# First mixer: early modulation tiles in places of their own, another order of parts and turnings, later tiles loaded sooner and summed one tile later

## The chip, the core and the metric

The kernel runs on one core of a Trainium2 chip. The metric is the device time of one execution in microseconds (us). TensorE is called PE here (its weight loads PEld), VectorE DVE, ScalarE ACT, GpSimd POOL, and SyncE SP; SP issues nearly all transfers from HBM. A "line" such as L1755 is a line of the kernel before, if nothing else is said.

## What is computed

Two transformer-like blocks on 256 tokens of width 1024 in float32. The change touches only the first thing that the kernel does: the modulation vectors and the first mixer up to its gates. Cut to that part:

```python
mod = jax.nn.silu(c) @ w_mod[i] + b_mod[i]            # 1024 -> 6144
sh1, sc1, g1, sh2, sc2, g2 = jnp.split(mod[:, None, :], N_MOD, axis=-1)
mod_c = jax.nn.silu(c_ctx) @ w_mod[i] + b_mod[i]      # the same for the context
h_lat = rms_norm(x_lat, norm1_g[i]) * (1.0 + sc1) + sh1
h_ctx = rms_norm(x_ctx, norm1_g[i]) * (1.0 + csc1) + csh1
...
q, v, zf, zb, g = jnp.split(h @ w_in, N_HG_PROJ, axis=-1)   # h: both, 512 rows
x_lat = x_lat + g1 * y_lat                                  # y_lat: the mixer's output
h2_lat = rms_norm(x_lat, norm2_g[i]) * (1.0 + sc2) + sh2    # then experts, then block two
```

## The kernel before

There is no scheduler: each engine's program is written out by hand, in order, and semaphores join them. An engine that waits holds everything behind it in its own program, and this is also true of SP, whose program is the list of transfers.

**Weight tiles.** All weights of the projections come as tiles of 1 MB (128 x 2048 float32) through three places, `raw0` to `raw2`. For each, ACT makes a rounded copy `whi` (L1244), DVE the rest `wlo` (L1755), and PE multiplies with both (three matmuls for each product). `whi` and `wlo` have four places each, and the split of a tile is written three tiles ahead of its use (`take`). A tile's load waits until the tile before it in the same place has been split. Counted from the first projection, weight tiles 0 to 3 are q (48 matmuls of 256 columns each), 4 to 7 are v (48 matmuls of 512 columns each), 8 and 9 are the first gates z0 and z1, and so on.

**Early modulation.** Columns 0 to 2047 of `w_mod` (sh1 and sc1) are eight 1 MB tiles. They are items of the same list, go through the same three places ahead of weight tile 0, and are used whole: PE multiplies the four rows of `CS` with them (`mod_rows`, L655, part c = 0 to 3 with two tiles each), ACT copies the 4 x 512 result out (L1338), PE turns it (`mod_cols`, L664) and DVE sums and adds the bias. PE turns the latent rows (`X`) and the context rows (`XC`) with `norm` (L642), ACT squares them (L1255), DVE scales (L1953), modulates (L1960) and, with ACT (L1270) and POOL (L2544), splits them into `HH` and `HL`. Then q0 may start.

**Later modulation.** Columns 2048 to 5119 are twelve 1 MB tiles, here called modulation tiles 0 to 11, in four places of their own in `ARENA` (`MRAW`, `load_mod`, L501). ACT multiplies a tile in place by the vector c (`products`, four instructions at L1318). When two neighbouring tiles (2s, 2s+1) are done, POOL adds them in three instructions (`row_sums`, L2557, L2559, L2562). This document calls the six results S4 to S9, by their column block: S4 comes from tiles 0 and 1, S5 from 2 and 3, S6 from 4 and 5, up to S9 from 10 and 11. PE folds each over the partitions (`mod_sums`, L676 for S4 and S5, L674 for the others) and DVE takes it over (`mod_cols`, L1867 or L1862). Modulation tiles 4 and 5 go to the places of 0 and 1, and their load therefore waits for S4; 6 and 7 wait for S5, 8 and 9 for S6, 10 and 11 for S7.

**The end of v.** The v projection fills banks 0 to 3 in weight tiles 4 and 5. Before tile 6 may start, DVE must have copied banks 0 and 2 (L2015), and ACT 1 and 3 (L1365). In DVE's program the copies stand behind the split of weight tile 8 and the take-over of S5.

**The gates.** ACT's first gate `unit_gate(0)` (L1288) waits for S9 and z0; z1 needs banks that it frees.

The two lines that tie the streams are, in SP's and POOL's programs:

```python
elif n >= 4:
    sp.wait_ge(*pmod.at("tile", n - 4))      # load_mod: n-4 is freed by its sum
...
if i == 14 or 16 <= i < 20:                  # i counts the 8 early tiles too:
    n = 2 if i == 14 else 2 * i - 28         # weight tile 6 behind modulation tiles 2, 3;
    load_mod(n)                              # 8 behind 4, 5; 9 behind 6, 7; ...
    load_mod(n + 1)
```

Of the kernel before, what the change touches and what calls it, by code (L numbers as in the profile page):

```python
# [114 lines left out]
MOD_SUMS = ((4,), (5,), (6,), (7,), (8, 9))  # L115
# [3 lines left out]
def weights(I):  # L119
# [14 lines left out]
    wm, wi = I["w_mod"][0], I["hg_w_in"][0]  # L134
    whole = set()

    def mod(c):
        whole.update((len(items), len(items) + 1))
        plan(wm, 0, 4, 512 * c, 512)
        plan(wm, 4, 4, 512 * c, 512)  # L140
# [7 lines left out]
    for c in range(4):  # L148
        mod(c)
# [68 lines left out]
    return items, base, whole  # L218


def build(nc, I, out, table):

    with ExitStack() as ctx:
# [19 lines left out]
        s_ld = [sem(f"raw{i}_landed") for i in range(NR + 2)]  # L243
        first, rows, xin, consts = (Landed(sem(n)) for n in ("first_landed", "rows_landed", "x_landed", "consts_landed"))
        gateb, router, fgl = (Landed(sem(n)) for n in ("gate_landed", "router_landed", "final_g_landed"))
# [28 lines left out]

        items, base, whole = weights(I)
        split_items = [i for i in range(len(items)) if i not in whole]
        turn_of = {i: n for n, i in enumerate(split_items)}


# [14 lines left out]
        due, n = [], NS - 1  # L294
        for i in range(len(items)):
            before = sum(1 for j in split_items[:n] if j < i)
            due.append([])
            while (n < len(split_items) and n < before + NS
                   and all(w < i for w in whole if w <= split_items[n] - NR)):
                due[i].append(n)  # L300
                n += 1
# [4 lines left out]
        for k, group in enumerate(PARAMS):  # L306
            r = 0
            for what, n in group:
                col.setdefault(what, at + r)
                r += n  # L310
            pt.append((ar(5000 if k == 0 else 7000 + 128 * k, 128), r, at))
            at += r
# [11 lines left out]
        FT, FTC = eight(ar(2048, 2048)), eight(ar(8192, 2048))  # L324
# [6 lines left out]
        MRS = [MR[:, :], ar(5400, 512)[0:4, :]]  # L331
# [19 lines left out]
        MRAW = [ar(o, 2048) for o in (10240, 6144, 8192, 12288)]  # L351
        MACC = [ar(14336, 512), G2B[:, 0:512]]
# [113 lines left out]
        def sync_program(sp):  # L466
            state, moe = {}, base["moe"]

            def load(i):
# [8 lines left out]
                if held[i] is not None:  # L478
                    sp.wait_ge(*(prj.at("item", held[i]) if held[i] in whole else wlow(held[i])))
                elif place[i] >= NR:  # L480
                    sp.wait_ge(*mm.at("mod_late", 11, 1))
                sp.dma_start(raw[place[i]][:, :].rearrange("p (k n) -> p k n", k=nk), src).then_inc(s_ld[place[i]], 16)

            def load_mod(n):
# [6 lines left out]
                elif n == 1:  # L491
                    sp.wait_ge(*vps.at("columns", 4))
                elif n == 2:
                    sp.wait_ge(*vlo.at("n", "hg_c", 2))
                    sp.wait_ge(*plo.at("n", "hg_c", 3))
                elif n == 3:
# [9 lines left out]

            sp.dma_start(CST[:, C_ID:C_ID + 128], I["consts"][:, C_ID:C_ID + 128]).then_inc(*first())
# [54 lines left out]
        def tensor_program(pe):  # L562
            state = {"next": 0, "late": 0}

            def take():
# [3 lines left out]
                if i in whole:  # L569
                    pe.wait_ge(s_ld[place[i]], 16 * had[i])  # L570
                    return i, [raw[place[i]][:, :].rearrange("p (k n) -> p k n", k=nk)]
                pe.wait_ge(*wlow(i))
                return i, [w[turn_of[i] % NS][:, :].rearrange("p (k n) -> p k n", k=nk) for w in (whi, wlo)]
# [59 lines left out]
            def norm(stage, xs, before=None, late=False):  # L633
                for q in range(4):
# [3 lines left out]
                    b = banks.next(pe, RING, "norm", stage, q)  # L638
# [9 lines left out]
            def mod_rows(c):  # L648
                b = banks.next(pe, SIDE, "mod_rows", c)
                if c == 0:  # L650
                    pe.wait_ge(*vec.at("cs"))
                for half in range(2):
                    i, (w,) = take()
                    for k in range(4):
                        x = pe.matmul(bank[b][0:4, :], f32(CSv[:, 4 * half + k, :]), w[:, k, :], start=half == 0 and k == 0,  # L655
                                      stop=half == 1 and k == 3)
                    x.then_inc(*prj("item", i))
                prj.also("mod_rows", c)

            def mod_cols(c):  # L660
                b = banks.next(pe, SIDE, "mod_cols", c)
                pe.wait_ge(*act.at("mod_rows", c))
                for k in range(4):
                    x = pe.transpose(bank[b][:, 4 * k:4 * k + 4], MRS[c % 2][:, 128 * k:128 * k + 128], ident[0:4, 0:4])  # L664
# [97 lines left out]
            def hgrn():  # L762
# [3 lines left out]
                pe.wait_ge(*xin.all(4))  # L766
                norm("hg_x", X, late=True)
# [1877 lines left out]
```

## Time and profile before

| | |
|---|---|
| three runs, median (lowest to highest) | 2089.04 us (2087.76 to 2092.61) |
| the profiled execution | 2090.62 us |
| its span in the trace | 2089.0 us |
| first matmul of the projections (q0) | 59.93 us after the span's start |
| first matmul of weight tile 6 | 121.29 us |
| first matmul of z1 | 159.88 us |

Between the profiled execution's time and its span lie 1.6 us. All times of the trace are counted from the span's start. In rows of a timeline the columns are start, duration, engine, line, operation, out<-in, shape and count, and in square brackets how long the engine sat idle and what ended it. "Chain" rows are the work that ended last, followed back: start, duration, what.

### The profile page before, as it was taken

To read this page: it belongs to the slowest core of one execution; us is meant where nothing else is said; L and a number is where in the kernel's file an instruction comes from. 1 tells how busy PE (TensorE), PEld (TensorE's weight loads), DVE (VectorE), ACT (ScalarE), POOL (GpSimd) and SP (SyncE) were. 2 spreads that over 40 slices of the span, in tenths; PEclk is the share of its full clock that TensorE was granted. 3 is DMA by queue.
4 is the path that set the end of the run, shared out by engine and by line. 5 is a ranking of instruction groups with operands and counts; after the bars stand their busy time and mean duration, and the time that the engine had idled before them with its cause. 6 is when DMAs were issued, how large, how long until landed. Compare 5 with 4: busy or idle time off the path is not lost.

```text
span 2089.0 us, 29140 instructions
## 1 busy us (share of the span) xinstructions
PE 1972.5 (94%) x12305; PEld 1737.2 (83%) x12305; DVE 1313.9 (63%) x1599; ACT 1036.7 (50%) x1211; POOL 89.7 (4%) x42
## 2 busy tenths in 40 slices
PE   7799989999989999999988999999999999999998
PEld 2678888698979888999877899897799988888997
DVE  1637765578876466665697655646655575567554
ACT  2656764377764455433535433445433344555332
POOL 0390000000000000000000000000000000000000
PEclk9899999899999999999999999999999999999999
DMA  6681125398964544565430456551365555345562
GB/s 233 245 300 42 60 80 195 102 343 301 308 214 162 181 142 161 165 199 182 151 121 22 160 182 194 173 182 61 104 197 183 194 170 181 122 161 180 183 191 82
DMA packets 230060, 355.55 MB, mean 170 GB/s; under 512 B 7058, under 2 KB 179883, under 8 KB 229675
## 3 DMA queue, kind: packets, MB, share of 16 engines
q1 hardware_dynamic: 229378, 353.47, 51.3%
q8 instruction: 98, 1.61, 0.3%
q10 hardware_dynamic: 552, 0.22, 0.0%
q14 instruction: 32, 0.25, 0.0%
HBM read 352.62 MB, written 1.05 MB: 169 GB/s over the span
## 4 chain that ended last, share of the span: by engine, by line
PE 83%; DVE 8%; ACT 4%; DMA 2%; issue 1%; POOL 0%; SPq 0%; ACTq 0%; DVEq 0%; POOLq 0%
PE bank L576 12%; PE bank L577 12%; PE bank L578 12%; PE bank L593 11%; PE bank L594 11%; PE bank L595 11%; DVE wlo L1755 2%; PE bank L1101 2%; ACT whi L1244 1%; DVE ARENA L2367 1%; DMA raw<-in_hg_w_in 1%; PE bank L655 1%; ACT ARENA L1255 1%; PE bank L858 1%; PE bank L837 1%
## 5 line engine op out<-in xcount | busy, mean ns | idle before, releaser
L1755 DVE TENSOR_TENSOR wlo<-raw,whi 128x2048 fp32r<-128x2048 f32 x282 | 653.2, 2320 | 348.2 <-ACT whi L1244 347.8
L1244 ACT CAST whi<-raw 128x2048 fp32r<-128x2048 f32 x282 | 535.4, 1903 | 224.8 <-PE bank L578 205.6
L593 PE MATMUL bank<-HH,whi 128*128 128x256 f32 (+1 forms) x2048 | 605.6, 296 | 15.3 <-DVE HL L1802 9.4
L594 PE MATMUL bank<-HL,whi 128*128 128x256 f32 (+1 forms) x2048 | 597.5, 292 | 0.0
L595 PE MATMUL bank<-HH,wlo 128*128 128x256 f32 (+1 forms) x2048 | 597.3, 292 | 0.0
L593 PEld LDWEIGHTS bank<-HH,whi 128*128 128x128 f32 x2048 | 397.1, 194 | 27.8 <-issue 14.0
L594 PEld LDWEIGHTS bank<-HL,whi 128*128 128x128 f32 x2048 | 397.3, 194 | 8.9 <-issue 1.9
L595 PEld LDWEIGHTS bank<-HH,wlo 128*128 128x128 f32 x2048 | 396.7, 194 | 5.1
L576 PE MATMUL bank<-whi,YH 128*128 128x512 f32 x816 | 320.8, 393 | 7.0 <-DVE YL L2411 5.6
L577 PE MATMUL bank<-wlo,YH 128*128 128x512 f32 x816 | 319.2, 391 | 0.0
L578 PE MATMUL bank<-whi,YL 128*128 128x512 f32 x816 | 318.1, 390 | 0.0
L576 PE MATMUL bank<-whi,HH 128*128 128x256 f32 (+1 forms) x544 | 183.4, 337 | 6.3 <-DVE ARENA L2015 3.1
L576 PEld LDWEIGHTS bank<-whi,YH 128*128 128x128 f32 x816 | 153.9, 189 | 37.5 <-DVE YL L2411 6.0
L578 PEld LDWEIGHTS bank<-whi,YL 128*128 128x128 f32 x816 | 153.7, 188 | 32.7
L578 PE MATMUL bank<-whi,HL 128*128 128x256 f32 (+1 forms) x544 | 179.0, 329 | 0.0
L577 PE MATMUL bank<-wlo,HH 128*128 128x256 f32 (+1 forms) x544 | 179.0, 329 | 0.0
L1531 ACT ACTIVATE YH<-ARENA 128x512 fp32r<-128x512 f32 x64 | 40.6, 634 | 278.6 <-DVE ARENA L2253 278.6
L577 PEld LDWEIGHTS bank<-wlo,YH 128*128 128x128 f32 x816 | 154.0, 189 | 28.4
L576 PEld LDWEIGHTS bank<-whi,HH 128*128 128x128 f32 x544 | 104.1, 191 | 21.8 <-issue 10.1
L577 PEld LDWEIGHTS bank<-wlo,HH 128*128 128x128 f32 x544 | 104.2, 192 | 9.6 <-issue 0.5
L578 PEld LDWEIGHTS bank<-whi,HL 128*128 128x128 f32 x544 | 104.1, 191 | 9.3
L2544 POOL TENSOR_TENSOR HL<-ARENA,HH 128x512 fp32r<-128x512 f32 x20 | 28.1, 1409 | 1799.4 <-ACT HH L1270 1799.4
(361 smaller groups left out, 1921.5 us busy)
## 6 DMA issues: line engine op xcount, KB each, us to landing
raw<-in_ffn_w SPq DMA_DIRECT2D x128, 1024.0 KB, 5.5
raw<-in_ret_w_in SPq DMA_DIRECT2D x48, 1024.0 KB, 5.2
raw<-in_hg_w_in SPq DMA_DIRECT2D x20, 1024.0 KB, 5.3
ARENA<-in_w_mod SPq DMA_DIRECT2D x16, 1024.0 KB, 7.5
raw<-in_ret_w_out SPq DMA_DIRECT2D x16, 1024.0 KB, 5.0
raw<-in_moe_w_gate SPq DMA_DIRECT2D x13, 1024.0 KB, 7.2
raw<-in_moe_w_up SPq DMA_DIRECT2D x13, 1024.0 KB, 7.4
raw<-in_moe_w_down SPq DMA_DIRECT2D x12, 1024.0 KB, 7.4
```

The lines of the kernel that those rows point to most:

```text
L576: pe.matmul(ps, lh, rh, start=start, stop=False)
L577: pe.matmul(ps, lh, rl, start=False, stop=False)
L578: return pe.matmul(ps, ll, rh, start=False, stop=stop)
L593: pe.matmul(ps, w[0][:, k, c], ah, start=begin, stop=False, skip_group_check=True)
L594: pe.matmul(ps, w[0][:, k, c], al, start=False, stop=False, skip_group_check=True)
L595: x = pe.matmul(ps, w[1][:, k, c], ah, start=False, stop=k == 7, skip_group_check=True)
L655: x = pe.matmul(bank[b][0:4, :], f32(CSv[:, 4 * half + k, :]), w[:, k, :], start=half == 0 and k == 0, stop=half == 1 and k == 3)
L1101: x = pe.matmul(bank[bf][:, c:c + 256], DG[:, n % NDG, :], HP[:, f, w:w + 256], start=w == (9 if f == 5 else 0), stop=w == 30)
L1244: ac.copy(whi[n % NS][:, :], raw[place[i]][:, :]).then_inc(*whi_("w", i))
L1531: ac.activation(yslot(j)[0], TG[j % 2], ACT.Square).then_inc(*ahi(st, "y", j))
L1755: ve.tensor_tensor(wlo[n % NS][:, :], raw[place[i]][:, :], f32(whi[n % NS][:, :]), SUB).then_inc(*wlv("w", i))
L2544: po.tensor_tensor(dst[1][:, kk, :], ft[:, kk, :], f32(dst[0][:, kk, :]), SUB).then_inc(*plo("n", stage, q))
```

## The change

What it does, part by part:

1. The eight early tiles of `w_mod` are no longer items of the weight list. They get eight places (`MFIRST`: the three `raw` places and five stretches of `ARENA`) and are all issued at the start, without waits. `raw` is first given to weight tiles once `mod_rows` has read it.
2. The order of the four parts is 0, 2, 1, 3 (`MOD_FIRST`): the first halves of shift and scale come first, and DVE normalizes and modulates the first half of the columns ahead of the second. The latent rows (`X`) wait for themselves alone. The context rows are loaded behind weight tile 0, turned on PE behind q0, and scaled and modulated on DVE behind the split of weight tile 3; all four of their low parts are on DVE, none on POOL.
3. The constants row groups 1 to 4 (`columns`) are turned ahead of the second part.
4. Modulation tiles 0 to 3 are loaded ahead of weight tile 4, and tiles 4 and 5, 6 and 7, 8 and 9, 10 and 11 each ahead of weight tiles 6, 7, 8 and 9.
5. ACT's `products`: tiles 0, 1 behind q0 (before: behind q2), 2, 3 behind q1 (q3), 4, 5 behind q3, where the split of weight tile 6 stands right ahead (before: behind the split of tile 7), then 6, 7 behind the split of tile 7, 8, 9 behind tile 8's and 10, 11 behind tile 9's.
6. PE folds S4 ahead of weight tile 4 (before: behind it), S5 behind tile 4, S6 behind 5, S7 behind 6, S8 behind 7, S9 behind z0.

The core of the diff:

```diff
-MOD_SUMS = ((4,), (5,), (6,), (7,), (8, 9))
+MOD_FIRST = (0, 2, 1, 3)
+MOD_SUMS = ((4,), (5,), (6,), (7,), (8,), (9,))
...
+        MFIRST = [r[:, :] for r in raw[0:3]] + [ar(o, 2048) for o in (0, 10240, 6144, 8192, 4096)]
...
             load_rows(sp, 0, first)
-            for i in range(NR):
-                load(i)
+            load_first(0)
+            load_first(1)
             for i in range(2):
                 sp.dma_start(X[i], I["x"][0, 128 * i:128 * i + 128, :]).then_inc(*xin())
+            load_first(2)
+            load_first(3)
+            load(0)
             for i in range(2):
-                sp.dma_start(XC[i], I["ctx"][0, 128 * i:128 * i + 128, :]).then_inc(*xin())
-            for i in range(NR, 13):
-                load(i)
+                sp.dma_start(XC[i], I["ctx"][0, 128 * i:128 * i + 128, :]).then_inc(*cin())
+            load(1)
             load_mod(0)
             load_mod(1)
+            load(2)
+            load_mod(2)
+            load(3)
             sp.dma_start(CST[:, 128:], I["consts"][:, 128:C_END]).then_inc(*consts())
+            load_mod(3)
+            for i in range(4, 6):
+                load(i)
...
-            for i in range(13, len(items)):
-                if i == 14 or 16 <= i < 20:
-                    n = 2 if i == 14 else 2 * i - 28
+            for i in range(6, len(items)):
+                if 6 <= i < 10:
+                    n = 2 * i - 8
                     load_mod(n)
                     load_mod(n + 1)
...
                 for j in range(4):
                     proj_b(("q", j), H16, 256, "hg_x" if j == 0 else None)
-                pe.wait_ge(*vlo.at("n", "hg_c", 2))
-                pe.wait_ge(*plo.at("n", "hg_c", 3))
+                    if j == 0:
+                        pe.wait_ge(*cin.all(2))
+                        norm("hg_c", XC, late=True, apart=SIDE)
+                        rms_rows("hg_c")
+                pe.wait_ge(*consts.all(1))
+                for n in MOD_SUMS[0]:
+                    mod_sums(n)
+                pe.wait_ge(*vlo.at("n", "hg_c", 3))
...
-                        for n in MOD_SUMS[2 * c + half]:
+                        for n in MOD_SUMS[2 * c + half + 1]:
                             mod_sums(n)
...
-                    if j == 0:
+                    if j == 2:
                         norm("hg_c", HC, shifted=True, late=True, ft=FTC)
-                    if j >= 2:
-                        products(2 * j - 4)
-                        products(2 * j - 3)
+                    if j != 2:
+                        n = (0, 1, 1, 2)[j]
+                        products(2 * n)
+                        products(2 * n + 1)
                 for c in range(2):
                     for half in range(2):
                         take()
-                        products(4 + 4 * c + 2 * half)
-                        products(5 + 4 * c + 2 * half)
+                        if 2 * c + half < 3:
+                            products(6 + 4 * c + 2 * half)
+                            products(7 + 4 * c + 2 * half)
```

The front of ACT's program, behind the first part's copy:

```diff
+                mod_out(0)
+                ac.wait_ge(*xin.all(2))
                 sum_squares(X, "hg_x")
                 rstd("hg_x")
+                mod_out(1)
+                mod_out(2)
+                normed(0)
+                normed(1)
+                split(0)
+                ac.wait_ge(*cin.all(2))
                 sum_squares(XC, "hg_c", 4)
...
+                mod_out(3)
+                normed(2)
+                normed(3)
                 split(1)
                 split(2)
+                rstd("hg_c")
```

**Where instructions stand, before and now.** SP's program from weight tile 5 on, before (a load with 4x512 into `raw` is a v tile, one with 8x256 a gate tile, one into `ARENA` a modulation tile; `pool_modulation` is POOL's sum):

```order
L482 DMA raw1<-in_hg_w_in 128x4x512 [waits dve_weight_lo]
L501 DMA ARENA<-in_w_mod 128x4x512 [waits pool_lo,dve_lo]
L501 DMA ARENA<-in_w_mod 128x4x512 [waits act_other,pe_transpose]
L482 DMA raw2<-in_hg_w_in 128x4x512 [waits dve_weight_lo]
L482 DMA raw0<-in_hg_w_in 128x4x512 [waits dve_weight_lo]
```

SP's program now, behind the load for `SM`:

```order
L485 DMA ARENA<-in_w_mod 128x4x512 [waits pool_modulation] x2
L469 DMA raw0<-in_hg_w_in 128x4x512 [waits dve_weight_lo]
L485 DMA ARENA<-in_w_mod 128x4x512 [waits pool_modulation] x2
L469 DMA raw1<-in_hg_w_in 128x4x512 [waits dve_weight_lo]
L485 DMA ARENA<-in_w_mod 128x4x512 [waits pool_modulation] x2
L469 DMA raw2<-in_hg_w_in 128x8x256 [waits dve_weight_lo]
```

Weight tiles 6 and 7 (the two last rows before, raw0 and raw1 now) stood ahead of the first wait for POOL; now tile 6 stands behind one pair that waits for POOL, tile 7 behind two, and tile 8 (raw2, 8x256) behind three. Before, tile 8 stood behind one.

ACT's program from the products of modulation tiles 2 and 3 on, before (`mod0` to `mod3` are the four places of modulation tiles; `whi` and `raw` numbers are places):

```order
L1318 ACTIVATE ARENA<-ARENA,SM 128x512 [waits mod3_landed]
L1318 ACTIVATE ARENA<-ARENA,SM 128x512 x3
L1244 CAST whi3<-raw0 128x2048 [waits pe_project,raw0_landed]
L1318 ACTIVATE ARENA<-ARENA,SM 128x512 [waits mod0_landed]
L1318 ACTIVATE ARENA<-ARENA,SM 128x512 x3
L1318 ACTIVATE ARENA<-ARENA,SM 128x512 [waits mod1_landed]
```

ACT's program now, from behind q2's silu on:

```order
L1270 CAST HH<-ARENA 128x2x256 [waits dve_other] x4
L1245 CAST whi2<-raw0 128x2048 [waits pe_project,raw0_landed]
L1364 ACTIVATE ARENA<-bank5 128x512 [waits pe_project]
L1318 ACTIVATE ARENA<-ARENA,SM 128x512 [waits mod0_landed]
L1318 ACTIVATE ARENA<-ARENA,SM 128x512 x3
L1318 ACTIVATE ARENA<-ARENA,SM 128x512 [waits mod1_landed]
```

The products of tiles 4 and 5 stood behind the split of weight tile 7 (whi3 from raw0); now they stand behind the split of weight tile 6 (whi2 from raw0) and q3's silu.

DVE's program around the copies out of banks 0 and 2, before:

```order
L1755 TENSOR_TENSOR wlo3<-raw0,whi3 128x2048 [waits act_weight_hi]
L1867 TENSOR_TENSOR G1B<-G1B,bank5 128x512 [waits gate_landed,pe_transpose]
L1755 TENSOR_TENSOR wlo0<-raw1,whi0 128x2048 [waits act_weight_hi]
L1867 TENSOR_TENSOR G1B<-G1B,bank6 128x512 [waits gate_landed,pe_transpose]
L2015 COPY ARENA<-bank0 128x512 [waits pe_project]
```

and now:

```order
L1769 TENSOR_TENSOR wlo3<-raw1,whi3 128x2048 [waits act_weight_hi]
L1879 TENSOR_TENSOR G1B<-G1B,bank7 128x512 [waits gate_landed,pe_transpose]
L1769 TENSOR_TENSOR wlo0<-raw2,whi0 128x2048 [waits act_weight_hi]
L1874 TENSOR_TENSOR SM<-bank4,PRM 128x4 [waits pe_transpose]
L2046 COPY ARENA<-bank0 128x512 [waits pe_project]
```

In both the copy stands behind the split of weight tile 8 (into wlo0); the sum that is taken over between them is now S6 (L1874) and was S5 (L1867).

## Rows read from the trace of the kernel before

**Rows 1.** The page: its span and busy time.
```profile
span 2089.0 us, 29140 instructions
PE 1972.5 (94%) x12305; PEld 1737.2 (83%) x12305; DVE 1313.9 (63%) x1599; ACT 1036.7 (50%) x1211; POOL 89.7 (4%) x42
```

**Rows 2.** Waits of PE from 60 to 260 us: total, times, longest.
```profile
PE bank L676 <- POOL ARENA L2562: 6.8, 1, 6.8
...
PE bank L576 <- DVE ARENA L2015: 3.1, 1, 3.1
```

**Rows 3.** Timeline of PE: early parts, a turning, q0, z1.
```profile
9.65 8.53 PE L655 MATMUL bank<-raw,CS 128*4 128x512 f32 x16 [3.82 <-DMA raw<-in_w_mod]
...
36.16 1.97 PE L642 MATMUL bank<-CST,ARENA 128*128 128x128 f32 x16
...
46.32 7.03 PE L655 MATMUL bank<-raw,CS 128*4 128x512 f32 x16
...
59.93 0.55 PE L593 MATMUL bank<-HH,whi 128*128 128x256 f32 x1 [5.45 <-DVE HL L1967]
...
159.88 0.47 PE L593 MATMUL bank<-HH,whi 128*128 128x512 f32 x1 [0.52 <-ACT ARENA L1289]
```

**Rows 4.** Busy time in a stretch of 5 us: five engines, clock, DMA share, GB/s.
```profile
15.00:20.00 5.00, 3.18 (x8) 0.52 (x6) 0.00 (x0) 0.00 (x0) 0.00 (x0) 1.00 1.03 379
```

**Rows 5.** Timeline of ACT: silu of q0, products of modulation tiles 0, 1 and 4.
```profile
76.89 0.60 ACT L1351 ACTIVATE ARENA<-bank 128x512 f32<-128x512 f32 x1
...
87.08 5.00 ACT L1318 ACTIVATE ARENA<-ARENA,SM 128x512 f32<-128x512 f32 x8
...
107.76 2.57 ACT L1318 ACTIVATE ARENA<-ARENA,SM 128x512 f32<-128x512 f32 x4 [5.30 <-DMA ARENA<-in_w_mod]
```

**Rows 6.** The chain that ended last, from 0 to 260 us: start, duration, what.
```profile
22.75 0.73 ACT ARENA L1255 x2
...
134.05 0.79 PE bank L674 x8
...
145.89 0.79 PE bank L674 x8
```

**Rows 7.** The same chain, from 92 to 122 us.
```profile
92.16 4.61 POOL ARENA L2557
...
96.84 4.28 POOL ARENA L2559
...
101.20 1.28 POOL ARENA L2562
...
103.46 9.91 DMA raw<-in_hg_w_in
...
113.39 1.93 ACT whi L1244
...
115.38 4.49 issue
...
120.54 0.61 DVE ARENA L2015
...
121.29 0.47 PE bank L576
```

**Rows 8.** Timeline of DVE: splits, the context's modulation.
```profile
56.90 2.28 DVE L1755 TENSOR_TENSOR wlo<-raw,whi 128x2048 fp32r<-128x2048 f32 x1
...
66.73 2.67 DVE L1960 TENSOR_SCALAR ARENA<-ARENA,SM 128x256 f32<-128x256 f32 x8
...
115.34 4.61 DVE L1755 TENSOR_TENSOR wlo<-raw,whi 128x2048 fp32r<-128x2048 f32 x1 [9.96 <-ACT whi L1244]
```

**Rows 9.** Timeline of POOL: its additions of S5 and S6.
```profile
109.31 2.40 POOL L2559 TENSOR_TENSOR ARENA<-ARENA 128x1024 f32<-128x1024 f32 x1
...
113.19 4.60 POOL L2557 TENSOR_TENSOR ARENA<-ARENA 128x2048 f32<-128x2048 f32 x1
117.87 4.30 POOL L2559 TENSOR_TENSOR ARENA<-ARENA 128x1024 f32<-128x1024 f32 x1
```

More of the change, by code:

```diff
@@ L273, in build @@
         twice = lambda ap: ap.rearrange("p (m n) -> p m n", m=1).to_broadcast([128, 2, 256])
-        items, base, whole = weights(I)
-        split_items = [i for i in range(len(items)) if i not in whole]
-        turn_of = {i: n for n, i in enumerate(split_items)}
+        items, base = weights(I)
         place, held, had, turns, newest = [], [], [], list(range(NR)), {}
@@ L293, in build @@
             had.append(place.count(turns[-1]))
[L294 to L301, printed above, removed]
         wlow = lambda i: wlv.at("w", i)
@@ L568, in take @@
                 nk = items[i][1]
-                if i in whole:
-                    pe.wait_ge(s_ld[place[i]], 16 * had[i])
-                    return i, [raw[place[i]][:, :].rearrange("p (k n) -> p k n", k=nk)]
                 pe.wait_ge(*wlow(i))
-                return i, [w[turn_of[i] % NS][:, :].rearrange("p (k n) -> p k n", k=nk) for w in (whi, wlo)]
+                return i, [w[i % NS][:, :].rearrange("p (k n) -> p k n", k=nk) for w in (whi, wlo)]
             def mm3(ps, lh, ll, rh, rl, start, stop):
@@ L631, in rms_rows, with norm @@
                 x.then_inc(*mm("rms", stage))
-            def norm(stage, xs, before=None, late=False):
+            def norm(stage, xs, before=None, late=False, apart=()):
                 for q in range(4):
@@ L646, in norm, with mod_rows, mod_cols @@
                     rms_rows(stage)
-            def mod_rows(c):
+            def mod_rows(j):
+                c = MOD_FIRST[j]
                 b = banks.next(pe, SIDE, "mod_rows", c)
-                if c == 0:
+                if j == 0:
                     pe.wait_ge(*vec.at("cs"))
[L652 to L660, printed above, removed]
+                pe.wait_ge(s_modf[j], 32)
+                for k in range(8):
+                    w = MFIRST[2 * j + k // 4][:, 512 * (k % 4):512 * (k % 4) + 512]
+                    x = pe.matmul(bank[b][0:4, :], f32(CSv[:, k, :]), w, start=k == 0, stop=k == 7)
+                x.then_inc(*prj("mod_rows", c))
+            def mod_cols(j):
+                c = MOD_FIRST[j]
                 b = banks.next(pe, SIDE, "mod_cols", c)
@@ L777, in hgrn @@
                     columns(k)
+                mod_rows(1)
+                pe.wait_ge(*xin.all(2))
+                norm("hg_x", X, late=True)
+                mod_cols(0)
+                mod_cols(1)
+                mod_rows(2)
+                rms_rows("hg_x")
                 mod_rows(3)
@@ L1759, in take @@
                 for _ in range(count):
-                    i = state["next"]
                     state["next"] += 1
-                    for n in due[i]:
-                        split(n)
+                    split(state["next"] + NS - 2)
             def own(ins):
@@ L1968, in low_part, with scales_of @@
                         *vlo("n", stage, q))
-                take(8)
-                normalized(0)
-                normalized(1)
-                mod_cols(0)
-                mod_cols(1)
+                def scales_of(half):
+                    for v in range(2):
+                        o = 8 * v + 4 * half
+                        sc = MODT[:, 1, :].rearrange("p (t v) -> p v t", v=2)[:, v, 4 * half:4 * half + 4]
+                        own(ve.scalar_tensor_tensor(MS[:, o:o + 4], sc, 1.0, prm("norm1_g", 4 * half, 4), ADD, MUL))
                 for k in range(1, 5):
                     columns(k)
+                rstd("hg_x", "hg_x")
+                mod_cols(0)
                 mod_cols(2)
-                mod_cols(3)
-                for v in range(2):
-                    sc = MODT[:, 1, :].rearrange("p (t v) -> p v t", v=2)[:, v, :]
-                    own(ve.scalar_tensor_tensor(MS[:, 8 * v:8 * v + 8], sc, 1.0, prm("norm1_g", 0, 8), ADD, MUL))
+                scales_of(0)
+                ve.wait_ge(*mm.at("rms", "hg_x"))
+                ve.tensor_copy(RBC[:, :], bank[0][:, 0:256]).then_inc(*vps("rms", "hg_x"))
+                banks.free(("rms", "hg_x"), vps)
+                ve.wait_ge(*vps.last())
+                normalized(0)
                 modulated(0, 0)
@@ L1989, in hgrn @@
                 split(1)
-                for q in range(4):
-                    modulated(1, q)
                 split(2)
@@ L2004, in hgrn @@
                 take()
-                low_part(1, 0)
-                low_part(1, 2)
-                take(3)
+                ve.wait_ge(*mm.at("rms", "hg_c"))
+                ve.tensor_copy(RBC[:, :], bank[0][:, 0:256]).then_inc(*vps("rms", "hg_c"))
+                banks.free(("rms", "hg_c"), vps)
+                ve.wait_ge(*vps.last())
+                normalized(1)
+                for q in range(4):
+                    modulated(1, q)
+                take(2)
+                for q in range(4):
+                    low_part(1, q)
+                take()
+                for n in MOD_SUMS[0]:
+                    mod_cols(n)
                 for c in range(2):
@@ L2010, in hgrn @@
                         take()
-                        for n in MOD_SUMS[2 * c + half]:
+                        for n in MOD_SUMS[2 * c + half + 1]:
                             mod_cols(n)
```

116 lines of the change are left out of this document (55 added, 61 removed).

## The prediction

> **What bounds the kernel now.** I read the page first: PE is busy 94% of 2089.0 us [rows 1], so a change to the start can give or take only idle time of PE, and the rest of the program follows as a block. I place the end of what the change touches at the first matmul of z1, 159.88 us [rows 3]. Behind it no instruction changes its place, and both kernels need S9 and z0 there. So the sum is: by how much does that matmul move?
>
> Next the waits of PE and its timeline. Ahead of q0 PE is tied to the early modulation and the scaled rows: q0 starts at 59.93 after 5.45 us of waiting for DVE [rows 3]. Behind it there are two waits worth counting: 6.8 us for POOL's S4, and 3.1 us for DVE's copy out of bank 0 [rows 2]. The second looks small, but the chain that ended last runs through it [rows 7]: POOL's three instructions of S4 (92.16 to 102.48), then the transfer of weight tile 8, then its rounding on ACT, its rest on DVE, the copy, and weight tile 6 on PE at 121.29. A DVE copy that needs nothing but v0 and v1 stands behind a weight tile that had to queue behind two modulation tiles, and those had waited for POOL. From the end of S4 to PE's start it is 121.29 - 102.48 = 18.8 us: 10.9 to the landing (113.39 is where ACT starts on the tile), 1.9 on ACT, 4.6 on DVE, and 1.3 for S5's take-over and the copy.
>
> **Part 1, the start: a gain.** PE takes the first early tile at 9.65 [rows 3]; the rest follow at 379 GB/s [rows 4], 2.8 us for each 1.05 MB. The first part now waits for both tiles, 12.4 us, and takes 8.5 us as in the row with the cold start, the three others 7.0 each [rows 3]. Their tiles are there in time (the eighth at about 32 us, the fourth part begins about 39). With some 4 us of turnings among them (2.0 for X [rows 3], the others smaller) the last part ends at 12.4 + 8.5 + 21.1 + 4 = 46 us, before at 53.35. ACT, however, now has the split of weight tile 0 and the four squares of the context (4 x 0.73 [rows 6]) ahead of the last part's copy; I put q0 at 50.5 us, 9.4 earlier.
>
> **Part 2, POOL's start: a larger gain.** Products of modulation tiles 0 and 1 ended at 92.08, POOL began at 92.16 [rows 5, 7]. Silu of q0 was at 76.89 [rows 5], 23.5 us behind the last part's end. In that stretch the change adds the squares (+2.9) and a second root (+0.8), takes the context's modulation out (-2.7 [rows 8]), and moves the first half's scaling, modulation and split under the last part (-2.3 for the split [rows 8], about -2 for the rest). That leaves 20.3, so silu of q0 is at about 66.5, and with 0.6 and 5.0 us behind it [rows 5] the products end near 72 to 73.4. POOL's S4 costs 4.6 + 2.4 + 1.3 = 8.3 us undisturbed. It was 10.3, because DVE's split and POOL's addition do not overlap: POOL's 2.40 becomes 4.30, and DVE's 2.28 becomes 4.61 while POOL is in its 4.60 [rows 8, 9]. Now two splits (weight tiles 4 and 5) and the context's four low parts fall into S4. Undisturbed S4 would end at 81.7, with every DVE instruction ahead of POOL at 88. The rows show both sides waiting, so I take two splits: 86.0. That is 16.5 us sooner than 102.48.
>
> **Part 3, the order of loads: the loss.** The copy out of bank 0 still stands behind the split of weight tile 8. But tile 8 now stands in SP's program behind modulation tiles 8 and 9, which wait for S6; before it stood behind 4 and 5, which wait for S4. And S6 has moved away from S4. Its products (tiles 4 and 5) stand on ACT behind the rounding of weight tile 6, whose load in turn stands behind modulation tiles 4 and 5 on SP. Step by step from the end of S4, with the durations of before:
>
> - three tiles issued and landed, the weight tile last: 10.9 us [rows 7]
> - ACT rounds weight tile 6: 1.9 [rows 7]; silu of q3: 0.6; products of 4 and 5: 5.1 [rows 5]. Before, they ran at 107.76, as soon as the modulation tile had landed [rows 5]
> - POOL's S6: 8.3, and 2.2 more for one split (tile 7) in it; hand-overs 0.1
>
> So S6 = S4 + 29.2 (27.0 with no split in it) = 115.2. Then the same trip a second time: 10.9 to the landing of weight tile 8, 1.9 on ACT, 2.3 on DVE (POOL waits for products then, so I take the undisturbed price; with it in the way 4.6), 1.0 for S6's take-over and the copy: 16.1 us. Weight tile 6 starts on PE at 131.3, 10.0 us **later** than 121.29. PE needs v0 and v1 ahead of it: S4's fold at 87, the context's low parts about 89, then twice 11.05 us (145.89 - 134.05 - 0.79 [rows 6]) and the folds. That is about 115: PE would stand some 16 us, and what PE gained at the start is idle time here.
>
> From weight tile 6 to z1 the work is the same: tiles 6, 7 and z0, two folds between them (0.79 each [rows 6]), the slow first matmuls after a wait in both. S9 was no limit before; now it ends near 153, ahead of z0's end, near 168. So z1 moves by +10.0.
>
> The trip is also where the Trainium skill has a price of its own. "DMA: Bandwidth & Descriptors", section on the anatomy of one DMA, puts a transfer at about 2.0 us plus its bytes over 436 GB/s. An estimate from it for three tiles in a row is 9.2 us instead of the measured 10.9; over two trips the change would cost 3.4 us less, 2095.6. The page's fit is for transfers that GpSimd issues, and the row is this queue's own, so the measured one is in the sum.
>
> **The sum.** Only PE's last link counts: -16.5 (S4) + 29.2 (S6 behind S4) + 16.1 (second trip) - 18.8 (the one trip of before) = +10.0 us. Against the profiled execution, 2090.62 (1.6 more than its span), that is 2100.6; against the median of the runs, 2089.04, it is **2099.0 us**.
>
> The parts with one answer: the turning of the constants is the same four instructions earlier; all eight places for early tiles cost no instruction; four low parts on DVE instead of two are 1.4 us on an engine that then waits for weight tile 6 anyway; the new wait for the root of the context ahead of q1 holds PE for 1 to 2 us, hidden by the stand further on.
>
> **Rivals.**
>
> *Faster.* The long chain does not hold PE, because POOL or the queue is much quicker than I put it, and PE is bound by its own work. Then tile 6 starts near 113 to 115, and z1 moves by -6 to -8: 2082. For it: everything ahead of S4 is earlier. Against it: tile 6 starts ahead of 121.29 only if S6 is done by 105.2, thus S4 by 78.2 even with no split inside S6. The products alone end at 72, and 8.3 must follow. The Trainium skill's rule of thumb (the same page, rules for kernel authors) is to issue a DMA early, so that its cost overlaps; by it the earlier modulation tiles would be this gain. Here a tile issued early is a tile that others queue behind. I give this 7%.
>
> *About the same, or slightly slower.* The chain holds as I say, but DVE and POOL hardly meet: S4 ends at 81.7, S6 27.0 later, tile 6 at 124.8. With the start 1 us quicker too, z1 moves by +2.5: 2091.5. I give results within 4.2 us of the median 11% in all. For it: POOL's six sums were never all disturbed (one 2.40 among them). Against it: two splits must fall in S4, because S4 starts just as weight tile 4 has been rounded.
>
> *Still slower.* DVE keeps ahead of POOL through its low parts (S4 at 88), and the split of tile 8 meets POOL (4.6): +14.3, 2103. I give it 20%, inside "slower".
>
> *The change does not do what it says.* If q0 did not start earlier, because ACT or the row constants are late, all of it would slide by up to 9 more. I see no wait in the listing for that: 3%.
>
> **Numbers.** Chances: my forecast (2095 to 2102) 59%, still slower 20%, the last rival 3%, about the same 11%, faster 7%. A measurement of this kernel can tell about 0.2%, 4.2 us, from no change. Faster by more than that: 0.07; within it: 0.11; slower: 0.82. The range of 80% reaches from 2091 (no meeting of POOL and DVE) to 2104.
>
> **What the profile would show.** Right: q0 at 49 to 52 us; S4's last POOL instruction ending at 83 to 88; ACT idle for some 15 us ahead of rounding weight tile 6 and again ahead of tile 8; weight tile 6 of PE waiting over 10 us for the DVE copy, at 129 to 133; z1 at 167 to 172. Wrong: if that copy is not the last thing that tile 6 waits for, if modulation tiles do not delay the weight tile behind them by about 5 us, or if POOL is idle for less than 5 us ahead of S6. And if tile 6 starts late as I say but the time is not longer, then PE caught up further on, which I have excluded.

## The result, and the profile after

| | before | after |
|---|---|---|
| median (lowest to highest), 7 runs each | 2089.05 us (2087.72 to 2092.61) | 2095.12 us (2092.75 to 2097.82) |
| after / before | | 1.0028, 95% interval 1.0017 to 1.0040 |
| the profiled execution, and its span | 2090.62, 2089.0 us | 2095.05, 2093.7 us |
| first matmul of q0 | 59.93 us | 49.43 us |
| last instruction of S4 on POOL ends | 102.48 us | 82.26 us |
| first matmul of weight tile 6 | 121.29 us | 126.57 us |
| first matmul of z1 | 159.88 us | 165.17 us |

The change makes the kernel 6.1 us slower. The forecast was 10.0 us slower, 2099.0, with a range that holds 2095.1. The table already tells the story: 10.5 us won at q0, 20.2 us won at S4, and 5.3 us lost at weight tile 6.

The first matmuls of q0 and of z1 in PE's timeline after (compare [rows 3]):

```profile
49.43 0.39 PE L589 MATMUL bank<-HH,whi 128*128 128x256 f32 x1
...
165.17 0.47 PE L589 MATMUL bank<-HH,whi 128*128 128x512 f32 x1 [0.43 <-DVE SM L1874]
```

The page after (compare [rows 1]): PE does the same matmuls, and the span is longer.

```profile
span 2093.7 us, 29142 instructions
PE 1968.0 (94%) x12305; PEld 1733.5 (83%) x12305; DVE 1323.3 (63%) x1603; ACT 1035.9 (49%) x1211; POOL 83.6 (4%) x40
```

The waits of PE after, from 50 to 260 us (total, times, longest; compare [rows 2]):

```profile
PE bank L572 <- DVE HL L1979: 9.9, 1, 9.9
PE bank L572 <- DVE ARENA L2046: 6.7, 1, 6.7
...
PE bank L675 <- POOL ARENA L2593: 4.4, 1, 4.4
```

Three waits take the place of two (6.8 and 3.1 before). L572 is the v projection: PE waits 9.9 us for the context's low parts ahead of v0, and 6.7 us for the copy out of bank 0 ahead of weight tile 6; 4.4 us are for S4, ahead of its fold. The chain that ended last, after, shows where the wait of 6.7 us comes from (start, duration, what; compare [rows 7]):

```profile
71.52 4.80 POOL ARENA L2588
76.39 2.40 POOL ARENA L2590
78.86 3.40 POOL ARENA L2593
...
83.26 9.56 DMA raw<-in_hg_w_in
...
95.23 4.91 ACT ARENA L1318 x8
100.28 4.59 POOL ARENA L2588
104.95 2.41 POOL ARENA L2590
107.43 3.23 POOL ARENA L2593
...
111.64 9.87 DMA raw<-in_hg_w_in
121.53 1.91 ACT whi L1245
123.46 2.29 DVE wlo L1769
125.83 0.61 DVE ARENA L2046
126.57 0.76 PE bank L572
```

Read it from the top. POOL makes S4; its end lets SP issue modulation tiles 4 and 5, and behind them weight tile 6 (the DMA at 83.26). ACT must round that tile before its products of 4 and 5 (95.23). Then POOL makes S6, SP issues 8 and 9 and behind them weight tile 8 (111.64), ACT and DVE split it, and only then comes the copy that PE waits for. The round trip "sum, transfer, ACT" stands in the chain twice. Before it stood there once.

### The profile page after: what moved, and what is told of

Same layout as the page of the kernel before. It is cut to its first block, busy times and chain, and to the rows that moved or that the text cites. A ratio compares the mean times of both kernels' runs of the same rounds, so it can differ in the third digit from the quotient of the medians.

```text
span 2093.7 us, 29142 instructions
## 1 busy us (share of the span) xinstructions
PE 1968.0 (94%) x12305; PEld 1733.5 (83%) x12305; DVE 1323.3 (63%) x1603; ACT 1035.9 (49%) x1211; POOL 83.6 (4%) x40
## 4 chain that ended last, share of the span: by engine, by line
PE 81%; DVE 9%; ACT 5%; DMA 2%; issue 2%; POOL 1%; SPq 0%; ACTq 0%; DVEq 0%; POOLq 0%
PE bank L572 12%; PE bank L573 12%; PE bank L574 12%; PE bank L589 11%; PE bank L590 11%; PE bank L591 11%; DVE wlo L1769 3%; PE bank L1103 2%; ACT whi L1245 2%; DVE ARENA L2398 1%; PE bank L655 1%; ACT ARENA L1255 1%; DMA raw<-in_hg_w_in 1%; PE bank L860 1%; PE bank L839 1%
## 5 line engine op out<-in xcount | busy, mean ns | idle before, releaser
L572 PE MATMUL bank<-whi,YH 128*128 128x512 f32 x816 | 320.8, 393 | 7.0 <-DVE YL L2442 5.6
L572 PE MATMUL bank<-whi,HH 128*128 128x256 f32 (+1 forms) x544 | 183.6, 337 | 20.1 <-DVE HL L1979 9.9
L572 PEld LDWEIGHTS bank<-whi,YH 128*128 128x128 f32 x816 | 153.9, 189 | 37.5 <-DVE YL L2442 6.0
L572 PEld LDWEIGHTS bank<-whi,HH 128*128 128x128 f32 x544 | 104.3, 192 | 36.3 <-DVE HL L1979 11.5
L2284 DVE SCALAR_TENSOR_TENSOR ARENA<-bank,RBC 128x512 f32<-128x512 f32 x64 | 44.2, 691 | 86.6 <-PE bank L591 86.4
```

Of the source, the lines that this page charges most:

```text
L572: pe.matmul(ps, lh, rh, start=start, stop=False)
L2284: ve.scalar_tensor_tensor(tr, two(bank[b][:, :]), 0.0, rbc2, ALU.max, MUL).then_inc(*vps(st, j))
```

## The experiments

Six of the eight kernels start from one of the two kernels and change one or two things. e5 changes several at once, and e8 adds one thing to e5. z1 is the first matmul of z1 in the profiled execution; its shift is against 159.88. Each ratio is against runs of the kernel before on the same chip; e8 ran on another chip than e1 to e7.

| | z1 starts | shift of z1 | median | ratio to before (95%) |
|---|---|---|---|---|
| after | 165.17 | +5.3 | 2095.12 | 1.0028 (1.0017 to 1.0040) |
| e1, load order of before | 156.84 | -3.0 | 2086.41 | 0.9991 (0.9982 to 1.0000) |
| e2, copies ahead | 157.05 | -2.8 | 2088.76 | 1.0000 (0.9991 to 1.0009) |
| e7, both | 156.48 | -3.4 | 2087.98 | 0.9994 (0.9985 to 1.0004) |
| e3, products ahead | 161.80 | +1.9 | 2092.70 | 1.0018 (1.0009 to 1.0027) |
| e4, before with the new load order | | | 2160.21 | 1.0341 (1.0322 to 1.0360) |
| e6, e1 with one low part | 153.50 | -6.4 | 2083.15 | 0.9969 (0.9957 to 0.9982) |
| e5, context first | 150.30 | -9.6 | 2079.52 | 0.9954 (0.9941 to 0.9968) |
| e8, e5 with S9 on DVE | 145.05 | -14.8 | 2075.04 | 0.9929 (0.9916 to 0.9943) |

The times follow z1, but only to within 3 us. In the profiled executions the span moves by up to 2.1 us more or less than z1 does, and each median, against the runs of before beside it, comes out 0.5 to 2.8 us later than the shift of z1 says.

**e1: the load order alone.** The changed kernel, with the pairs of modulation tiles where they stood before, two weight tiles later:

```diff
-                if 6 <= i < 10:
-                    n = 2 * i - 8
+                if 8 <= i < 12:
+                    n = 2 * i - 12
```

> The changed kernel with one part undone: modulation tiles 4 to 11 are loaded ahead of weight tiles 8 to 11 again, so weight tiles 6 and 7 wait for no sum. Theory (the chain S4, loads, products 4 and 5, S6, loads, weight tile 8, DVE's copy holds weight tile 6 on PE): tile 6 starts on PE right behind v1, at about 118.9 us instead of 126.57, and the time falls by 7.7 us, to about 2087.4. Rival (the loss comes from DVE and POOL blocking each other, v0 starting late): v0 still starts at 94 and the time stays within 2 us of 2095.

Measured: 2086.41 us (2085.50 to 2090.68). In e1's waits of PE the copy is down to 0.9 us, and weight tile 6 starts at 120.85 (theory 118.9). The copy's wait, then the first matmul of v0 in its timeline:

```profile
PE bank L572 <- DVE ARENA L2046: 0.9, 1, 0.9
```
```profile
94.58 0.79 PE L572 MATMUL bank<-whi,HH 128*128 128x512 f32 x1 [9.96 <-DVE HL L1979]
```

So the wait for the copy is nearly gone, and the one ahead of v0 is there as in the changed kernel. The order of loads accounts for the whole loss: undoing it gives back 8.7 us. What is left of the change gains 2.5 us, which the interval (up to 1.0000) only just tells from nothing. It gains no more since v0 starts at 94.6, and PE then runs through v0 and v1 to the copies.

**e2 and e7: the copy alone, and both.** In e2 the load order stays, and DVE and ACT copy the banks of v ahead of the split of weight tile 8 instead of behind it (and ahead of that of tile 10):

```diff
                     for half in range(2):
+                        if half:
+                            ve.wait_ge(*prj.at("v", c))
+                            ... copies out of banks 0 and 2 (ACT: 1 and 3)
                         take()
```

> The changed kernel with its load order, but the copies out of banks 0 to 3 stand on DVE and ACT ahead of the split of weight tile 8 (and of tile 10) instead of behind it. Theory: the late landing of tile 8, near 121 us, no longer reaches PE; tile 6 starts near 119 and z0 (144) still comes after the split of tile 8 (126): about 2087.5. Rival (the loads themselves are late for PE, or POOL's S9 is the bound): 2093 to 2095.

Measured: 2088.76 us (2086.68 to 2090.41). In PE's waits the copy is missing altogether, and weight tile 8 still is issued late, in SP's timeline of e2 at 112.57 us:

```profile
111.61 0.92 SPq L485 DMA_DIRECT2D ARENA<-in_w_mod  x2
112.57 0.51 SPq L469 DMA_DIRECT2D raw<-in_hg_w_in  x1
```

So the late tile costs only through the copy that stands behind its split. e7 makes both edits:

> e1's load order and e2's earlier copies together in the changed kernel. Theory: they cut the same chain, so together they bring no more than one: tile 6 was already right behind v1 in both, only DVE's last 0.9 us goes: 2085.5 to 2088.5. Rival (two separate losses of some 6 to 8 us each): near 2080.

Measured: 2087.98 us (2087.03 to 2088.86). Each edit takes z1 from +5.3 to about -3, both together to -3.4. They cut the same chain at two links, and what bounds PE behind it is v0. z1 moved by -2.8 in e2, the median by -0.2 only; e1 kept 2.5 of its 3.0. The difference lies behind z1, and no run here explains it.

**e3: products ahead.** If the sum S6 is the trouble, ACT could make its products ahead of the split of weight tile 6:

```diff
                 for j in range(4):
+                    if j == 3:
+                        products(4)
+                        products(5)
                     take()
...
-                    if j != 2:
-                        n = (0, 1, 1, 2)[j]
+                    if j < 2:
+                        n = (0, 1)[j]
```

> The changed kernel with its load order, but ACT multiplies modulation tiles 4 and 5 ahead of rounding weight tile 6. Theory: the products run as soon as the tiles land (87.6 to 93), S6 ends at 103.5 instead of 110.7, weight tile 8 lands at 114.4 and the copy is done at 119.3; tile 6 starts near 119.6: about 2088. Rival (POOL's own time or the queue sets S6): S6 stays at 108 or later and the time above 2093.

Measured: 2092.70 us (2091.35 to 2094.40), a miss by 4.7 us. The chain did what was asked of it: S6 ended at 103.9 instead of 110.7. But now POOL has no pause between S5 and S6, and DVE loses by it. POOL and then DVE in e3:

```profile
82.05 6.43 POOL L2591 TENSOR_TENSOR ARENA<-ARENA 128x2048 f32<-128x2048 f32 x1
88.56 2.68 POOL L2593 TENSOR_TENSOR ARENA<-ARENA 128x1024 f32<-128x1024 f32 x1
91.32 1.59 POOL L2596 TENSOR_TENSOR G2B<-ARENA 128x512 f32<-128x512 f32 x1
93.00 4.83 POOL L2591 TENSOR_TENSOR ARENA<-ARENA 128x2048 f32<-128x2048 f32 x1
```
```profile
84.05 14.33 DVE L1982 TENSOR_TENSOR HL<-ARENA,HH 128x512 fp32r<-128x512 f32 x4
```

Four low parts, from 84.05 to 98.4, lie beside POOL's four additions of 82.05 to 97.8. PE waits for them 14.3 us instead of 9.9, and v0 starts at 98.43, 3.9 us later than in e1. Weight tile 6 starts at 125.80, 4.95 later than in e1; the last 1.1 us of that lie between v0 and tile 6 and were not traced.

**e4: the new load order in the kernel before.** The reverse of e1: pairs of modulation tiles ahead of weight tiles 5 to 9, and nothing else.

```diff
-                if i == 14 or 16 <= i < 20:
-                    n = 2 if i == 14 else 2 * i - 28
+                if 13 <= i < 18:
+                    n = 2 * i - 24
```

> The kernel before with one part done alone: the pairs of modulation tiles from 4 on stand two weight tiles earlier in SP's order (4, 5 ahead of weight tile 6, and so on; 2, 3 ahead of tile 5), nothing else. ACT's products of 2 and 3 stand behind the split of tile 6 here, so every sum waits for a weight tile that waits for the sum before. Theory: S4 at 102.5, tile 6 lands at 113.4, S5 near 131, S6 near 159, tile 8 lands near 170, weight tile 6 starts on PE near 176, and S9 near 227 holds the first gate: +55 to +70 us, 2145 to 2160. Rival (sooner loads are harmless or help): within 10 us of 2089.

Measured: 2160.21 us (2160.02 to 2160.40, two runs), 71 us slower, a little over the expected span. SP's timeline of e4:

```profile
82.20 0.93 SPq L501 DMA_DIRECT2D ARENA<-in_w_mod  x2
83.19 0.50 SPq L482 DMA_DIRECT2D raw<-in_hg_w_in  x1
109.61 0.92 SPq L501 DMA_DIRECT2D ARENA<-in_w_mod  x2
...
161.57 0.92 SPq L501 DMA_DIRECT2D ARENA<-in_w_mod  x2
```

and one turn of its chain:

```profile
83.19 10.75 DMA raw<-in_hg_w_in
...
96.37 4.89 ACT ARENA L1318 x8
101.33 4.50 POOL ARENA L2557
105.90 2.35 POOL ARENA L2559
108.32 1.27 POOL ARENA L2562
...
110.57 9.57 DMA raw<-in_hg_w_in
```

A pair is issued every 26.5 us (from 82.20 to 161.57 in three turns): transfer, split, products and sum in a ring. Weight tile 6 starts on PE at 177.96, after a wait of 39.9 us for the copy out of bank 0 (theory: near 176). In the kernel before, the products of tiles 4 and 5 stand behind the split of weight tile 7, those of 6 and 7 behind tile 8's; with the new load order that weight tile in turn stands behind a pair that waits for the sum just before. No two steps of the ring overlap. The changed kernel opens it by making each pair of products one split sooner, and is left with two turns ahead of the copy. The order of loads is worth as much as the order on ACT allows.

**e6: one instruction for the four low parts.** e1, and on DVE:

```diff
                 for q in range(4):
-                    low_part(1, q)
+                    ve.wait_ge(*ahi.at("n", "hg_c", q))
+                ve.tensor_tensor(HC[1], FTC, f32(HC[0]), SUB).then_inc(*vlo("n", "hg_c", 3))
```

> The kernel e1_loads_back (modulation pairs behind weight tiles 6 and 7) with one more edit: the context's four low parts on DVE, 128x512 each, are one instruction of 128x2048. With the loads back the next limit is the start of v0 at 94.6, held by the four low parts, which take 10.0 us for 2.7 us of work, since each of them waits for an addition of POOL. Theory (DVE pays per instruction, not per element, when POOL adds): one instruction waits once, is done near 91.3, v0 starts 3 us earlier and the time falls from 2086.4 to about 2083.5. Rival (the port is shared by the bytes moved): no change, 2086.

Measured: 2083.15 us (2079.97 to 2086.50). The rest of the context on DVE and v0 on PE, in e6:

```profile
84.50 6.58 DVE L2036 TENSOR_TENSOR HL<-ARENA,HH 128x2048 fp32r<-128x2048 f32 x1
```
```profile
91.14 0.80 PE L572 MATMUL bank<-whi,HH 128*128 128x512 f32 x1 [6.52 <-DVE HL L2036]
```

The same bytes take 6.58 us in one instruction and 10.02 in e1's four. v0 starts 3.4 us sooner, z1 3.3 us sooner, the median falls by 3.3 us. Here the price of meeting POOL was paid for each instruction, not for each byte.

**e5: the context ahead of POOL.** The load order of e1, the copies of e2, and: ACT's products of tile 1 wait until the context is rounded, so that DVE has modulated and split it before POOL begins; ACT's products of tiles 2 to 11 each stand one place later than in the changed kernel; PE folds S4 behind v1 instead of ahead of v0, and S5 to S8 one or two places later; the fourth early part's copy stands ahead of the context's squares on ACT. None of these was run alone.

```diff
-MOD_SUMS = ((4,), (5,), (6,), (7,), (8,), (9,))
+MOD_SUMS = ((), (4,), (5,), (6, 7), (8, 9))
...
-                    if j == 2:
+                    if j == 0:
+                        products(0)
                         norm("hg_c", HC, shifted=True, late=True, ft=FTC)
+                    if j == 1:
+                        products(1)
```

> A version built from what the runs showed: the changed kernel with the loads of e1, the copies out of banks 0 to 3 ahead of the splits of tiles 8 and 10, ACT's copy of the last early part ahead of the context's squares, the context's rounding and low parts done before POOL starts (ACT: products of tile 0, the context, split of tile 4, products of tile 1; DVE: low parts ahead of the splits of 4 and 5), and S4 folded behind v1 instead of ahead of v0. Theory: low parts end near 76, v0 starts right behind q3 at 78 to 80; POOL runs without a gap from about 78 to 142, S9 becomes the bound of the first gate, z1 starts near 144 instead of 159.9: about 2073. Rival (what was saved ahead is again lost behind, at another wait): above 2083.

Measured: 2079.52 us (2078.60 to 2080.63), faster than both kernels, but 6.5 us short of the time that was expected (about 2073). DVE's context work, in e5:

```profile
72.23 2.66 DVE L1972 TENSOR_SCALAR ARENA<-ARENA,SM 128x256 f32<-128x256 f32 x8
74.81 2.49 DVE L1979 TENSOR_TENSOR HL<-ARENA,HH 128x512 fp32r<-128x512 f32 x4
```

2.66 and 2.49 us, where the changed kernel has 9.14 and 9.99 (rows in the next section). v0 starts at 82.77 with no wait at all, 11.6 us sooner. Where did the rest go? The end of POOL's timeline and z1, in e5:

```profile
136.47 4.61 POOL L2590 TENSOR_TENSOR ARENA<-ARENA 128x2048 f32<-128x2048 f32 x1 [1.57 <-ACT ARENA L1316]
141.16 4.27 POOL L2592 TENSOR_TENSOR ARENA<-ARENA 128x1024 f32<-128x1024 f32 x1
145.50 1.26 POOL L2595 TENSOR_TENSOR G2B<-ARENA 128x512 f32<-128x512 f32 x1
```
```profile
150.30 0.77 PE L589 MATMUL bank<-HH,whi 128*128 128x512 f32 x1 [1.55 <-ACT ARENA L1287]
```

S9 was no limit before; here z0's products are done at 141.2 and the first gate stands until S9 ends at 146.76. POOL had begun at 80.38 and needs 66.4 us for the six sums, 12.4 for the first and 10.3 to 10.5 for each of the others, with hardly a pause.

**e8: S9 on DVE.** e5, with the three additions of the last sum on DVE, ahead of its last split there, and the gate's wait turned to them:

```diff
+                t0, t1, acc = MRAW[2], MRAW[3], MACC[1]
+                ve.wait_ge(*act.at("products", 11))
+                own(ve.tensor_tensor(t0, t0, t1, ADD))
+                own(ve.tensor_tensor(t0[:, 0:1024], t0[:, 0:1024], t0[:, 1024:2048], ADD))
+                own(ve.tensor_tensor(acc, t0[:, 0:512], t0[:, 512:1024], ADD))
+                vec.also("sums", 9)
                 take()
...
-            for c in range(4, 10):
+            for c in range(4, 9):
                 row_sums(c)
```

> The context-first version, with one thing changed: the last of the six sums (tiles 10 and 11) is made on VectorE instead of GpSimd, and the first gate unit waits for it there. In the context-first version's trace z0's products end at 141.6, but the sigmoids of z0 wait for GpSimd's last sum (136.47 to 146.76, three adds of 4.61, 4.27 and 1.26 us), so z1 starts at 150.30. Theory A (the 6 us that the context-first version fell short of its expectation, 2079.5 instead of 2073, are this wait, because GpSimd works back to back from 80.38 on and a sum takes 10.4 us there): on VectorE the three adds take an estimated 2.3 + 1.3 + 0.7 us (its rows of 128x2048 and 128x512) and end at 141, z1 starts at 143.5 to 145, and the time falls by 5 to 7 us, to 2072.5 to 2074.5. Theory B (the shortfall lies later in the program, in the places of the low granted clock, or the wait is only replaced, for instance by the split of z1's weight tile, which now stands behind the adds on VectorE): z1 starts later than 147 and the time stays within 2 us of 2079.5.

Measured: 2075.04 us (2070.07 to 2075.85). DVE and PE, in e8:

```profile
137.22 2.29 DVE L2053 TENSOR_TENSOR ARENA<-ARENA 128x2048 f32<-128x2048 f32 x1 [1.54 <-ACT ARENA L1317]
139.54 1.23 DVE L2054 TENSOR_TENSOR ARENA<-ARENA 128x1024 f32<-128x1024 f32 x1
140.80 0.69 DVE L2055 TENSOR_TENSOR G2B<-ARENA 128x512 f32<-128x512 f32 x1
```
```profile
145.05 0.77 PE L589 MATMUL bank<-HH,whi 128*128 128x512 f32 x1 [1.28 <-ACT ARENA L1288]
```

The sum takes 4.3 us instead of 10.3, z1 starts 5.25 us sooner, and the median falls by 4.5. Against the kernel before on its own chip, e5 is 9.1 us faster and e8 13.2, so the fall may be nearer 4.1. That is theory A in the main: z1 came at the late end of its range, and theory B had put it later than 147. But the fall is short of the 5 to 7 us that A gave; of the 6.5 us that e5 missed, some 2 stay unexplained. e8 is 13 us faster than the kernel before and 19 to 20 us faster than the changed one. It keeps the change's early tiles and early context; what it drops is the order of loads, and the order on ACT and DVE that let the sums meet the context.

## Why the prediction was right, and where it was off

The mechanism was right: the second trip through POOL, the queue and ACT is what makes weight tile 6 late. The size was too large, and the median came out only just inside the part of the range that I gave 59% (2095 to 2102). Of the profile's signs that I named, only the start of q0 came in its range. S4 ended at 82.26 (named: 83 to 88), weight tile 6 started at 126.57 (129 to 133) after a wait of 6.7 us (over 10), z1 at 165.17 (167 to 172), and ACT sat idle for 9.9 and 9.6 us ahead of weight tiles 6 and 8 (some 15). None of the signs of a wrong mechanism came: the copy was the last thing that tile 6 waited for; weight tile 6 landed 9.6 us after its issue behind the pair, where the quickest weight tile in e1 (60 to 112 us) took 5.1; and POOL was idle for 7.1 us ahead of S6.

**Part 1 held.** The last early part ended at 45.8 us (forecast 46), q0 started at 49.43 (50.5), the silu of q0 at 65.94 (about 66.5).

**Part 2 was mis-sized by 3.7 us; it is the term that explains most of the gap.** S4 was put at 86.0 and ended at 82.26. Two halves of about 2 us. POOL began at 71.52, since I had taken the later end of 72 to 73.4 for its start; and its three instructions took 10.7 us, not 12.6. I had charged POOL with both of DVE's splits. The rows of the changed kernel show how the two engines share; POOL, then DVE:

```profile
71.52 4.79 POOL L2588 TENSOR_TENSOR ARENA<-ARENA 128x2048 f32<-128x2048 f32 x1 [17.51 <-ACT ARENA L1318]
76.39 2.40 POOL L2590 TENSOR_TENSOR ARENA<-ARENA 128x1024 f32<-128x1024 f32 x1
78.86 3.40 POOL L2593 TENSOR_TENSOR ARENA<-ARENA 128x512 f32<-128x512 f32 x1
82.34 6.42 POOL L2588 TENSOR_TENSOR ARENA<-ARENA 128x2048 f32<-128x2048 f32 x1
```
```profile
69.79 9.14 DVE L1972 TENSOR_SCALAR ARENA<-ARENA,SM 128x256 f32<-128x256 f32 x8
78.86 5.55 DVE L1769 TENSOR_TENSOR wlo<-raw,whi 128x2048 fp32r<-128x2048 f32 x2
84.33 9.99 DVE L1979 TENSOR_TENSOR HL<-ARENA,HH 128x512 fp32r<-128x512 f32 x4
```

Two splits came at 78.86. The first held POOL's 1.28 us addition for 2.1 us; the second then stood behind that addition, and held the next one (6.42 instead of 4.6), which is S5 and no longer S4. In these rows an addition of POOL waits for at most one instruction of DVE, and the reverse. So only one split fell into S4.

**What the prediction did not see** is the other side of this: the context's modulation and low parts, 2.67 [rows 8] and 2.49 us (e5) alone, took 9.14 and 9.99. I had put v0 at 89; it started at 94.4. It changed nothing in the sum, because the chain through S6 ended later still, and PE waited in two places (9.9 and 6.7) where I had about 16 us in one. But in every experiment that cut the chain it was the next bound, and it made e3 miss.

**Part 3 held.** S6 behind S4: 28.4 us (forecast 29.2). The second trip, from S6's end at 110.65 to weight tile 6: 15.9 us (16.1). The forecast of z1 was 4.7 us too late: 3.7 of them are S4, 0.8 the way to S6, 0.2 the second trip. With the measured terms the sum is -20.2 + 28.4 + 15.9 - 18.8 = +5.3, which is what z1 shows: 165.17. That both trips pass through weight tiles 6 and 8 is shown by e1 and e2, each of which cuts one link.

The Trainium skill's price for the three queued tiles ("DMA: Bandwidth & Descriptors", anatomy of one DMA, an estimate of 9.2 us) does not agree: from SP's first issue at 82.29 to ACT's start on the weight tile at 92.84 it took 10.55 us, and 10.85 the second time (110.68 to 121.53). That the time worked out with it, 2095.6, lies next to the measured 2095.12 is chance: the gap was S4's, not the transfers'.

**Behind z1** I had excluded a change. The profiled span grew by 4.7 us, the medians by 6.1. At the first unit's matmuls (L705 now, L706 before) the wait for DVE is 1.59 instead of 0.83 us, which accounts for the shift of 6.1 there; further on the shift of PE's matmuls varies between 2.9 and 6.4 us in the one profiled execution (from 1200 us on it is 3.4), with stretches of a low granted clock at other places (the ten microseconds from 300 had 0.69 before and 0.81 after). What these are worth was not tested.

**The rivals.** "About the same" had S4 at 81.7 and S6 27.0 later; measured are 82.3 and 28.4, so the result lies between it and the forecast. That its S4 is so near is luck: it had POOL start at 73.4 and not meet DVE at all, and POOL started at 71.5 and lost 2.4 us by DVE. "Faster" and "still slower" did not occur. "Faster" had its condition named, S4 by 78.2: POOL's start at 71.5 leaves 6.7 us for 8.3 us of additions.

## What to carry to other kernels

When one queue carries two streams, write down for each load what its wait depends on, and whether that in turn needs something loaded behind it in the same queue: a tile moved ahead gains nothing if the tiles behind it inherit its wait, and a ring of wait, load, split, product and sum cost 26 us a turn here. When an early stage gets faster, look up which engine then meets which: here the sums moved on top of the context's work on DVE, and it was worth 3.3 us to make its small instructions one (e6 against e1) and 8.5 us to use an order in which they run ahead of the sums (e5 against e7; e5 also moves products and folds, so not all of it is shown to be the context's). Check two cuts of one chain separately and together before adding up their gains: e1 and e2 move z1 by 8 us each, and both together by 8.7.

## What the runs showed of the hardware

DVE and POOL took turns instruction by instruction in the rows where both worked from SBUF. Within the changed kernel, the durations of the four low parts (shortest, median, longest in ns, then first and last start) are:

```profile
L1979 DVE TENSOR_TENSOR HL<-ARENA,HH x4: 679/2284/4976, 84.3 to 93.6; 128x512 fp32r<-128x512 f32 x4
```

One takes 0.68 us alone (e5) and up to 4.98 us here: it stands behind a whole addition of POOL's (4.6 us alone), then runs, then POOL has its turn again. In order the four took 4.98, 2.82, 1.75 and 0.68 us, beside POOL's additions of 2048, 1024 and 512 columns and then none. In e3, where POOL went on with S6, the fourth took 4.98 too. So four instructions cost 9.99 to 14.33 us, one with the same bytes 6.58 (e6). DVE's instructions that read a bank of PSUM were not held: the take-over `G1B<-G1B,bank` took 0.68 us beside POOL (0.67 in e6 at 95.39, within an addition of POOL from 93.39 to 96.62).

The Trainium skill, "SBUF — State Buffer", section "SBUF: two separate sides", says that the pair of ports which the two share is an exclusive lock, held for the whole instruction, and that whichever starts first gets it; it names a DVE instruction with two inputs in SBUF, as the low parts and splits have, against one of GpSimd's that reads SBUF. The trace agrees that the loser waits in full (0.68 us became 4.98). Who is next when both have work is told here by the trace alone: the durations of the additions, splits and low parts above fit with one instruction of the other in between, each time.
